# Token columns reordered and padded: prompts first, samples behind them, 272 columns per chunk instead of 264

## The chip, the cores and the metric

The kernel runs on one core of a Trainium2 chip. The metric is the device time of one execution in microseconds. Three executions of the kernel before took 560.51, 561.38 and 562.12 us; their median, 561.38 us, is the time that the change is compared with.

## The reference: what is computed

One inference step of a decoder layer for 256 prompt tokens and 8 sample tokens with 1024 channels, all in float32. All 264 tokens share the weights, so the large products are done once for both groups.

```python
x = x + 0.5 * swiglu_ffn(x, ffn1_norm, ffn1_w_in, ffn1_w_out)     # 1024 -> 2*2816 -> 1024
h = rmsnorm(x, mix_norm)
u, q, k, v, qm = split(h @ w_in)                                  # 1024 -> 2048
y_pool = pool_mixer(u, ...)                                       # windows 2, 4, 8, 16
y_moba = moba_attention(rotary(rmsnorm(q)), k_past + k, v_past + v)   # 8 heads x 64
y_mem  = mem_attention(rmsnorm(qm), mk, mv)                       # 256 memory tokens, 4 heads
x = x + concat(y_pool, y_moba, y_mem) @ w_out                     # 1024 -> 1024
x = x + 0.5 * swiglu_ffn(x, ffn2_norm, ffn2_w_in, ffn2_w_out)
```

Besides x, the new keys and values, the memory keys and values and the pooling state are returned.

## The kernel before

**Activations lie transposed.** Channels are on the 128 partitions and tokens along the free dimension, so 1024 channels are 8 chunks of `[128, 264]` in `xT`, `x_hi` and `x_lo`, and the 2816 hidden channels are 22 such chunks in `h_hi` and `h_lo`. In each chunk the 8 samples are columns 0 to 7 and the 256 prompts columns 8 to 263.

**Each float32 product is three matmuls.** A value is split into a rounded part (`_hi`, type float32r) and the rest (`_lo`). `three` (lines 1505 to 1507) issues hi·hi, hi·lo and lo·hi into the same PSUM accumulation. ScalarE makes `w_hi` from the loaded weights `raw` (line 701), VectorE makes `w_lo` (line 1021).

**Units of weights.** The weights come in 512 KB units into a ring of four slots of `[128, 1024]`, each unit used in this way:

- FFN in (`ffn_unit`, 44 units in each FFN): eight weight blocks of 128 columns are the stationary operands, one for each of the eight x chunks, and the x chunk of 264 columns is the moving operand: 8 x 3 = 24 matmuls into one PSUM bank. The moving operand goes on to the next chunk every three matmuls. The first FFN takes the chunks in the order 0 to 7, the second in the order 4, 5, 6, 7, 0, 1, 2, 3 (`M_ORDER`). Two units of the second FFN, at its start, take the hi products of all chunks first (lines 1531 to 1535).
- FFN out (`outer`, 22 units in each FFN): one h chunk is the moving operand for all 24 matmuls of a unit, while the eight weight blocks and the eight PSUM banks change. The last two units are interleaved (`last_two`).
- The output projection of the mixer ("MIX", 8 units) is of the same kind, with x chunks in the order 0, 1, 4, 5, 6, 7 and then 2 and 3 interleaved.
- Memory keys and values: 48 matmuls in which memory chunks of 128 columns (`m_hi`, `m_lo`) are stationary and the weights, 512 columns wide, are moving.
- The projection `w_in` of the prompts (`project`, 192 matmuls): the same with x as the stationary operand: a block of 128 prompts, from column 8 or 136 of a chunk. Between these stand the products of the samples and of the attention.

**Order and waits.** All five engines run instruction streams written out by hand and tied by counted semaphores; in the middle part a table `EXTRA` and a list `TAIL` say what is placed between the projection's steps. The change leaves both alone. TensorE waits for `lo_ready` before a unit, ScalarE for `w_used` before it writes a ring slot again.

**Where the tensors lie.** `place` gives each tensor a byte offset in the partition, counted up from 1152 and rounded to 64. From the shapes: `raw` 1152, `w_hi` 17536, `w_lo` 33920, `xT` 50304, `x_hi` 58752, `x_lo` 67200, `m_lo` 141696, `m_hi` 149888, `h_hi` 181952, `h_lo` 205184. A chunk of 264 float32 columns is 1056 bytes, that is 16.5 times 64, so chunk k of `x_hi` starts at byte 58752 + 1056 k. Weight blocks of 128 columns (512 bytes) all have the same remainder in a division by 256.

**The per-token norm of the mixer** (step "SS"): TensorE sums squares over the partitions, into column 0 of a PSUM bank for the samples (once in each quarter of the partitions) and into columns 1 and 2 for the prompts, and ScalarE and VectorE take root and reciprocal of the whole 128 x 3 block.

Of the kernel before, what the change touches and what calls it, by code (L numbers as in the profile page):

```python
# [13 lines left out]
ds = bass.ds  # L14
# [7 lines left out]
NP = 256  # L22
N = NS + NP
POOL, MOBA, MEM = 256, 512, 256
HD = 64
# [85 lines left out]
def layer(nc, a):  # L111

    ctx = ExitStack()
    with ctx:
        cursor = [1152]

        def place(name, shape, dt=F32, at=None):
            size = 4 * int(np.prod(shape[1:]))
            if at is None:
                at = cursor[0]  # L120
                cursor[0] += -(-size // 64) * 64
            return nc.alloc_sbuf_tensor_at(name, list(shape), dt, offset=at)
# [46 lines left out]
        dummy = place("dummy", [P, 4])  # L169
        ms = place("ms", [P, 2])  # L170
        m_root = place("m_root", [P, 2])
        m_rstd = place("m_rstd", [P, 2])
        t_root = place("t_root", [P, 3])
        t_rstd = place("t_rstd", [P, 3])
        x_ss = place("x_ss", [P, 3])
        x_root = place("x_root", [P, 3])
        x_rstd = place("x_rstd", [P, 3])
        page_ids = place("page_ids", [1, NS * PAGES], I32)
# [14 lines left out]

        late_slot = place("late_slot", [P, PAGES * 512], at=cursor[0])
        q_cols = place("q_cols", [P, 4 * 513])
        region = cursor[0]
        late_end = region + 4 * PAGES * 512 - (-(-4 * 4 * 513 // 64) * 64)
# [109 lines left out]
        ALL, MEM_ROWS = slice(0, P), slice(64, P)  # L307


        def cols_view(w, k):  # L310
# [383 lines left out]
        def _(act):  # L694
# [196 lines left out]
            for what, k in steps():  # L891
# [54 lines left out]
                elif what == "HY":  # L946
                    c0 = (2, 4, 6)[k]
                    act.wait_ge(pv_done, 2 * k + 2)
                    act.activation(x_hi[:, c0:c0 + 2, NS:N], bank[HY_BANKS[k]].rearrange("p (c n) -> p c n", c=2), ACT.Copy).then_inc(hy_hi, 1)
                elif what == "A" and k == 3:  # L950
# [11 lines left out]
                elif what == "M" and k == 0:  # L962
                    act.wait_ge(smn_ready, 1)
                    act.activation(rows_m[:], bank[QM_BANK][:, 0:NP], ACT.Exp, scale=SCALE, bias=m_stats[:, 1:2],
                                   accum_out=m_stats[:, 2:3]).then_inc(sme_ready, 1)
                elif what == "M" and k == 2:
                    act.wait_ge(p_psum, 1)
                    act.activation(pm_cols[:].rearrange("p t c -> p (t c)"), bank[QM_BANK][:, 0:NP], ACT.Copy).then_inc(pcols_ready, 1)
                elif what == "YR":
                    act.wait_ge(v_used, V_DONE[k])  # L970
                    if k:
                        act.wait_ge(yr_psum, k)
                    if k < 2:
                        act.wait_ge(s_total, 1)
                        act.activation(y_rows_s[:], bank[V_BANKS[k]][:, :], ACT.Copy, scale=stats[:, 64 + k:65 + k]).then_inc(yr_ready, 1)
                    else:
                        act.activation(y_rows_s[:], bank[QM_BANK][:, :], ACT.Copy).then_inc(yr_ready, 1)
                elif what == "CAT":
                    act.wait_ge(ys_ready, 4 + 2 * k)
                    c0, c1 = ((2, 6), (6, 8))[k]  # L980
                    act.activation(x_hi[:, c0:c1, 0:NS], ys[:, c0:c1, :], ACT.Copy).then_inc(cat_hi, 1)
            for r in range(4, KT + 1):
# [17 lines left out]
            act.wait_ge(res_ready, 3 * KT)  # L1000
            act.activation(xs[:], xT[:, :, 0:NS], ACT.Copy).then_inc(xs_copied, 1)
            y_rows(act, 2)
# [5 lines left out]
        def _(vec):  # L1008
# [25 lines left out]
            def residual(inst, last, weight, g0):  # L1034
# [7 lines left out]
                for idx, m in enumerate(M_ORDER):  # L1042
# [6 lines left out]
                    if g0 is None and idx < 4:  # L1049
                        vec.wait_ge(res_ready, KT * inst + idx + 1)  # L1050
                        vec.transpose(y_square(idx), xT[:, m, NS:N]).then_inc(y_squares, 1)
                    if g0 is not None and idx:
# [9 lines left out]
            def up_hidden(f, c, s, n, b0=GU_BANK, split_of=None):  # L1062
# [3 lines left out]
                if split_of is not None:  # L1066
# [4 lines left out]
                vec.wait_ge(hm_ready, c + (HT * f + 1))  # L1071
                vec.tensor_copy(h_hi[:, ds(c, 1), :].rearrange("p a n -> p (a n)"), h_tmp[:, s, :]).then_inc(hhi_ready, 1)
                vec.wait_ge(hhi_ready, c + (HT * f + 1))
                vec.tensor_tensor(h_lo[:, ds(c, 1), :].rearrange("p a n -> p (a n)"), h_tmp[:, s, :],  # L1074
                                  h_hi[:, ds(c, 1), :].rearrange("p a n -> p (a n)").bitcast(F32), ALU.subtract)\
                    .then_inc(h_ready, 1)
# [245 lines left out]
            for what, k in steps():  # L1322
# [127 lines left out]
                elif what == "HY":  # L1450
                    c0 = (2, 4, 6)[k]
                    vec.wait_ge(hy_hi, k + 1)
                    vec.tensor_tensor(x_lo[:, c0:c0 + 2, NS:N], bank[HY_BANKS[k]].rearrange("p (c n) -> p c n", c=2),
                                      x_hi[:, c0:c0 + 2, NS:N].bitcast(F32), ALU.subtract).then_inc(hy_lo, 1)
                elif what == "POOL" and k == 1:
# [20 lines left out]
                elif what == "CAT":  # L1476
                    vec.wait_ge(cat_hi, k + 1)
                    c0, c1 = ((2, 6), (6, 8))[k]
                    vec.tensor_tensor(x_lo[:, c0:c1, 0:NS], ys[:, c0:c1, :], x_hi[:, c0:c1, 0:NS].bitcast(F32), ALU.subtract).then_inc(cat_lo, 1)
            for r in range(4, KT + 1):  # L1480
# [21 lines left out]
        def _(pe):  # L1502
# [36 lines left out]
            def row_norms():  # L1539

                for t in range(3):
                    n, c0 = (NS, P, P)[t], (0, NS, NS + P)[t]
                    pe.wait_ge(xwide_ready, t + 1)
# [22 lines left out]

            hidden = lambda k: tuple(h[:, ds(k, 1), :].rearrange("p a n -> p (a n)") for h in (h_hi, h_lo))

# [57 lines left out]
            def project_samples(r):  # L1626
# [81 lines left out]
            def sample_turns(half):  # L1708
                for m in range(4 * half, 4 * half + 4):
                    turn(bank[X_BANKS[m]][:, 0:NS], x_rows[0:NS, 0, m * P:(m + 1) * P], NS)  # L1710

            def prompt_turns(half):
                pe.wait_ge(x_loaded[half], 32)
                for m in range(4 * half, 4 * half + 4):
                    turn(bank[X_BANKS[m]][:, NS:NS + P], x_rows[:, 1, m * P:(m + 1) * P])
                    turn(bank[X_BANKS[m]][:, NS + P:N], x_rows[:, 2, m * P:(m + 1) * P]).then_inc(x_turned, 1)

# [49 lines left out]
            for what, k in steps():  # L1767
# [26 lines left out]
                elif what == "SS":  # L1794
                    pe.wait_ge(sum_step, KT - 1)
                    pe.wait_ge(qkT_ready, 1)
                    for q in range(4):
                        pe.matmul(bank[SS_BANK][32 * q:32 * q + 32, 0:1], tmp[:, M_ORDER[0], 0:32], ones[:, 0:1], start=True, stop=True)
                    for tt in (1, 2):
                        c0 = (0, NS, NS + P)[tt]  # L1800
                        mm = pe.matmul(bank[SS_BANK][:, tt:tt + 1], tmp[:, M_ORDER[0], c0:c0 + P], ones[:, 0:1], start=True, stop=True)
# [26 lines left out]
                elif what == "POOL" and k == 0:  # L1828
# [3 lines left out]
                    for pr in range(2):  # L1832
# [3 lines left out]
                        for g, r, u0, u1 in pair:  # L1836
                            pe.matmul(out[r, NS:NS + P], u0, band[:, g, 0:P], start=True, stop=True)
                        for g, r, u0, u1 in pair:
                            pe.matmul(out[r, NS + P:N], u1, band[:, g, P + EDGE:], start=True, stop=False)
                        for g, r, u0, u1 in pair:  # L1840
                            pe.matmul(out[r, NS + P:NS + P + EDGE], u0, band[:, g, P:P + EDGE], start=False, stop=True)
                        for g, r, u0, u1 in pair:
                            mm = pe.matmul(out[r, 0:NS], ext[:, g * HD:(g + 1) * HD], samp[:, g, :], start=True, stop=True)
                        mm.then_inc(pooled_psum, 1)
# [118 lines left out]
            for pair in range(2):  # L1963
                for q in range(2):
                    pe.wait_ge(res_ready, 2 * KT + 4 + (2 if pair == 0 else 3 + q))
                    for t in range(2):
                        mm = turn(bank[Y_BANKS[2 * pair + t]][:, q * P:(q + 1) * P], xT[:, 2 * pair + q, NS + t * P:NS + (t + 1) * P])
                        if q:
# [31 lines left out]
```

## Time and profile before

| | |
|---|---|
| median of three executions | 561.38 us (560.51 to 562.12) |
| span of the profiled execution, first to last instruction | 559.2 us |
| TensorE matmuls | busy 551.3 us (99%), 5075 of them |
| TensorE weight loads | 513.6 us (92%) |
| VectorE, ScalarE, GpSimd | 398.9 us (71%), 269.2 us (48%), 17.7 us (3%) |
| granted TensorE clock | 1.000 |
| DMA | 128.40 MB, mean 230 GB/s |

The profiled execution's own device time is not listed apart from its span. The span lies 2.2 us under the median, which is what lies around it when it is taken as one execution like the three.

The duration that the profile gives for a matmul runs from its issue to its last result. Matmuls overlap: the next one starts long before the last has ended. What a matmul costs in a dense stretch is the distance from its start to the start of the next, and this is read from the timeline, whose first column is the start; the busy time of a group divided by its count says nothing about it.

### The profile page before, as it was taken

How to read it: one execution, taken by the hardware profiler on the slowest of the kernel's cores; microseconds unless marked ns; L12 is line 12 of the kernel's file. 1: busy time of each engine (PE TensorE's matmuls, PEld its weight loads, DVE VectorE, ACT ScalarE, POOL GpSimd, SP SyncE). 2: the span in 40 equal slices, each digit the busy share in tenths (PEclk: the TensorE clock that was granted, in tenths of full speed). 3: DMA queues.
4: the chain of work that ended last, by engine and by line, in shares of the span. 5: the costliest groups of instructions: out<-in, count | busy, mean ns of one | idle time of the engine just before them, and what ended most of it. 6: DMA issues, size and time to landing. Idle time of an engine off the chain costs nothing.

```text
span 559.2 us, 13391 instructions
## 1 busy us (share of the span) xinstructions
PE 551.3 (99%) x5075; PEld 513.6 (92%) x5075; DVE 398.9 (71%) x715; ACT 269.2 (48%) x425; POOL 17.7 (3%) x24
## 2 busy tenths in 40 slices
PE   8999999999999999999999999999999999999997
PEld 8999999999899998666777679999999999999997
DVE  4687888885588877889946685689777777664444
ACT  5844464444543337344535785475444344433330
POOL 1000000000000003100000000140000000000000
PEclk9999999999999999999999999999999999999999
DMA  9799999784567664899999994566756666465523
GB/s 236 208 269 324 271 315 268 234 249 149 196 216 273 205 209 160 273 338 382 351 300 371 373 337 143 163 180 197 211 168 191 182 175 194 132 220 181 187 75 79
DMA packets 137481, 128.40 MB, mean 230 GB/s; under 512 B 10937, under 2 KB 108880, under 8 KB 137432
## 3 DMA queue, kind: packets, MB, share of 16 engines
q1 hardware_dynamic: 134703, 127.24, 72.8%
q10 hardware_dynamic: 2736, 0.61, 0.5%
q8 instruction: 26, 0.43, 0.3%
q14 instruction: 16, 0.12, 0.1%
HBM read 125.12 MB, written 2.83 MB: 229 GB/s over the span
## 4 chain that ended last, share of the span: by engine, by line
PE 85%; DVE 7%; DMA 3%; ACT 2%; issue 1%; SPq 0%; DVEq 0%; ACTq 0%
PE banks L1505 25%; PE banks L1506 25%; PE banks L1507 25%; PE banks L1665 3%; PE banks L1513 2%; DVE w_lo L1021 2%; PE banks L1939 1%; PE banks L1637 1%; DMA raw<-in_ffn_w_in 1%; PE banks L1890 1%; DMA x_rows<-in_x_sample 1%; DMA page_ids<-in_page_table 1%; PE banks L1866 1%; ACT x_hi L827 1%; DVE prob_pair L1448 1%
## 5 line engine op out<-in xcount | busy, mean ns | idle before, releaser
L701 ACT ACTIVATE w_hi<-raw 128x1024 fp32r<-128x1024 f32 x158 | 166.5, 1059 | 194.9 <-PE banks L1507 160.8
L1021 DVE TENSOR_TENSOR w_lo<-raw,w_hi 128x1024 fp32r<-128x1024 f32 x158 | 193.8, 1232 | 73.9 <-ACT w_hi L701 72.7
L1505 PE MATMUL banks<-x_hi,w_hi 128*128 128x264 f32 x752 | 214.1, 285 | 0.1
L1506 PE MATMUL banks<-x_lo,w_hi 128*128 128x264 f32 x752 | 213.0, 283 | 0.0
L1507 PE MATMUL banks<-x_hi,w_lo 128*128 128x264 f32 x752 | 213.0, 283 | 0.0
L1505 PEld LDWEIGHTS banks<-x_hi,w_hi 128*128 128x128 f32 x752 | 141.6, 188 | 0.7 <-issue 0.4
L1506 PEld LDWEIGHTS banks<-x_lo,w_hi 128*128 128x128 f32 x752 | 141.7, 188 | 0.0
L1507 PEld LDWEIGHTS banks<-x_hi,w_lo 128*128 128x128 f32 x752 | 141.0, 188 | 0.0
L1505 PE MATMUL banks<-h_hi,w_hi 128*128 (+1 forms) x352 | 100.2, 285 | 0.0
L1507 PE MATMUL banks<-h_hi,w_lo 128*128 (+1 forms) x352 | 100.2, 285 | 0.0
L1506 PE MATMUL banks<-h_lo,w_hi 128*128 (+1 forms) x352 | 100.0, 284 | 0.0
L1506 PEld LDWEIGHTS banks<-h_lo,w_hi 128*128 128x128 f32 x352 | 66.5, 189 | 0.0
L1505 PEld LDWEIGHTS banks<-h_hi,w_hi 128*128 128x128 f32 x352 | 66.2, 188 | 0.3 <-ACT mem_kv L879 0.3
L1507 PEld LDWEIGHTS banks<-h_hi,w_lo 128*128 128x128 f32 x352 | 66.3, 188 | 0.0
L1065 DVE TENSOR_TENSOR h_tmp<-banks,rstd 128x264 f32<-128x264 f32 x44 | 18.9, 429 | 22.7 <-PE banks L1507 22.7
L1032 DVE STREAM_TRANSPOSE kv<-kv 128x1024 f32<-128x1024 f32 x28 | 33.9, 1228 | 0.0
L1505 PE MATMUL banks<-w_hi,x_hi 128*128 128x512 f32 x64 | 28.0, 438 | 0.3 <-ACT qp L794 0.3
L726 ACT ACTIVATE sg<-sg 128x264 f32<-128x264 f32 x44 | 18.3, 415 | 18.2 <-DVE sg L1060 18.2
L1507 PE MATMUL banks<-w_hi,x_lo 128*128 128x512 f32 x64 | 25.3, 395 | 0.0
L1506 PE MATMUL banks<-w_lo,x_hi 128*128 128x512 f32 x64 | 25.2, 394 | 0.0
L1074 DVE TENSOR_TENSOR h_lo<-h_tmp,h_hi 128x264 f32 (+1 forms) x44 | 19.1, 434 | 3.6
L1070 DVE TENSOR_TENSOR h_tmp<-sg,h_tmp 128x264 f32<-128x264 f32 x44 | 19.0, 433 | 3.3 <-ACT sg L726 2.0
(287 smaller groups left out, 501.7 us busy)
## 6 DMA issues: line engine op xcount, KB each, us to landing
raw<-in_ffn_w_in SPq DMA_DIRECT2D x86, 512.0 KB, 4.8
raw<-in_ffn_w_out SPq DMA_DIRECT2D x44, 512.0 KB, 3.4
kv<-in_cache_k SPq DMA_DIRECT2D x56, 256.0 KB, 4.8
kv<-in_cache_v SPq DMA_DIRECT2D x48, 256.0 KB, 6.3
raw<-in_w_in SPq DMA_DIRECT2D x12, 512.0 KB, 5.2
late_slot<-in_cache_v SPq DMA_DIRECT2D x16, 256.0 KB, 4.6
raw<-in_w_out SPq DMA_DIRECT2D x8, 512.0 KB, 7.5
raw<-in_mem_w_kv SPq DMA_DIRECT2D x4, 512.0 KB, 4.0
```

The costliest lines, as they stand in the source:

```text
L701: act.activation(w_hi[:, n % RING, :], raw[:, n % RING, :], ACT.Copy).then_inc(hi_ready, 1)
L726: act.activation(sg[:, s, :], sg[:, s, :], ACT.Silu).then_inc(silu_ready, 1)
L1021: vec.tensor_tensor(w_lo[:, n % RING, :], raw[:, n % RING, :], w_hi[:, n % RING, :].bitcast(F32), ALU.subtract).then_inc(lo_ready, 1)
L1032: vec.transpose(key_pair(g), key_pair(g)).then_inc(k_turned8, 1)
L1065: vec.tensor_tensor(h_tmp[:, s, :], bank[b0 + 2 * s + 1][:, 0:N], rstd[:], ALU.mult).then_inc(gu_free, 1)
L1070: vec.tensor_tensor(h_tmp[:, s, :], sg[:, s, :], h_tmp[:, s, :], ALU.mult).then_inc(hm_ready, 1)
L1074: vec.tensor_tensor(h_lo[:, ds(c, 1), :].rearrange("p a n -> p (a n)"), h_tmp[:, s, :], h_hi[:, ds(c, 1), :].rearrange("p a n -> p (a n)") ...
L1505: pe.matmul(out, lhs[0], rhs[0], start=start, stop=False)
L1506: pe.matmul(out, lhs[0], rhs[1], start=False, stop=False)
L1507: return pe.matmul(out, lhs[1], rhs[0], start=False, stop=stop)
L1513: return pe.transpose(out, in_, ident[0:k, 0:k])
L1665: mm = pe.matmul(bank[LG_BANK][32 * hp:32 * hp + 32, half * NP:(half + 1) * NP], q_cols[:, c0:c0 + 32], keys[:, 4 * hp + c], start=(b4 == ...
```

## The change

Prompts are now columns 0 to 255 of each chunk and the samples columns 256 to 263. The chunks of `x_hi`, `x_lo`, `h_hi` and `h_lo` lie 272 columns (1088 bytes, 17 times 64) apart, while still 264 columns are computed; `xT` and `tmp` keep 264. `place` rounds to 32 bytes rather than 64 and counts two bytes for a bfloat16, and eight small tensors share one, to make room. Which columns each instruction reads or writes follows from this everywhere. One instruction is added: VectorE sets column 0 of the norm's PSUM bank to one, because the samples' sum is now written to 8 rows of each quarter rather than to 32.

New offsets that matter here: `x_hi` 58752 and the three weight tensors as before, `x_lo` 67456, `h_hi` 181440, `h_lo` 205376.

```diff
+PITCH = 272
+PROMPT, SAMPLE = slice(0, NP), slice(NP, N)
+TOKENS = ((NP, NS), (0, P), (P, P))
...
-            size = 4 * int(np.prod(shape[1:]))
+            size = (2 if dt == BF16 else 4) * int(np.prod(shape[1:]))
             if at is None:
                 at = cursor[0]
-                cursor[0] += -(-size // 64) * 64
+                cursor[0] += -(-size // 32) * 32
...
-        x_hi = place("x_hi", [P, KT, N], F32R)
-        x_lo = place("x_lo", [P, KT, N], F32R)
+        x_hi = place("x_hi", [P, KT, PITCH], F32R)[:, :, 0:N]
+        x_lo = place("x_lo", [P, KT, PITCH], F32R)[:, :, 0:N]
...
-        h_hi = place("h_hi", [P, HT, N], F32R)
-        h_lo = place("h_lo", [P, HT, N], F32R)
+        h_hi = place("h_hi", [P, HT * PITCH], F32R)
+        h_lo = place("h_lo", [P, HT * PITCH], F32R)
...
+        def hidden_of(h, c):
+
+            return h[:, ds(c * PITCH, N)]
...
+            vec.memset(bank[SS_BANK][:, 0:1], 1.0).then_inc(xs_ready, 1)
             vec.memset(bank[S_BANK][:, 0:P], 0.0).then_inc(xs_ready, 1)
             vec.wait_ge(res_ready, KT)
-            vec.tensor_tensor(xs[:], xT[:, :, 0:NS], gains[:, 8:16].unsqueeze(2).to_broadcast([P, KT, NS]), ALU.mult).then_inc(xs_ready, 1)
+            vec.tensor_tensor(xs[:], xT[:, :, SAMPLE], gains[:, 8:16].unsqueeze(2).to_broadcast([P, KT, NS]), ALU.mult).then_inc(xs_ready, 1)
...
-            hidden = lambda k: tuple(h[:, ds(k, 1), :].rearrange("p a n -> p (a n)") for h in (h_hi, h_lo))
+            hidden = lambda k: (hidden_of(h_hi, k), hidden_of(h_lo, k))
...
-                k, c0 = 2 * J_ORDER[r] + kk, (0, NS, NS + P)[tt]
+                k, c0 = 2 * J_ORDER[r] + kk, TOKENS[tt][0]
...
-                    pe.wait_ge(xs_ready, 2)
+                    pe.wait_ge(xs_ready, 3)
...
-                        pe.matmul(bank[SS_BANK][32 * q:32 * q + 32, 0:1], tmp[:, M_ORDER[0], 0:32], ones[:, 0:1], start=True, stop=True)
+                        pe.matmul(bank[SS_BANK][32 * q:32 * q + NS, 0:1], tmp[:, M_ORDER[0], SAMPLE], ones[:, 0:1], start=True, stop=True)
```

The instruction streams stay the same but for two places. On VectorE, behind the residual of the first FFN and ahead of the split of the projection's third weight unit, the kernel before has (banks are PSUM, `xs` the samples' columns):

```order
L1039 SCALAR_TENSOR_TENSOR x_lo<-xT,gains,x_hi 128x264 x2
L1315 MEMSET banks 128x128
L1317 TENSOR_TENSOR xs<-xT,gains 128x64
L1021 TENSOR_TENSOR w_lo<-raw,w_hi 128x1024
L1330 MEMSET q_spread 128x128
```

and the changed one:

```order
L1045 SCALAR_TENSOR_TENSOR x_lo<-xT,gains,x_hi 128x264 x2
L1320 MEMSET banks 128x1
L1321 MEMSET banks 128x128
L1323 TENSOR_TENSOR xs<-xT,gains 128x64
L1027 TENSOR_TENSOR w_lo<-raw,w_hi 128x1024
L1336 MEMSET q_spread 128x128
```

One memset of a single column has come in; nothing has moved past another. On TensorE, in the third step of the projection, where the squares are summed, there stood

```order
L1507 MATMUL banks<-w_hi,x_lo 128x512
L1818 MATMUL banks<-q_spread,joined 128x128
L1798 MATMUL banks<-ones,tmp 32x1 x4
L1801 MATMUL banks<-ones,tmp 128x1 x2
L1505 MATMUL banks<-w_hi,x_hi 128x512
```

and now stands

```order
L1513 MATMUL banks<-w_hi,x_lo 128x512
L1824 MATMUL banks<-q_spread,joined 128x128
L1804 MATMUL banks<-ones,tmp 8x1 x4
L1807 MATMUL banks<-ones,tmp 128x1 x2
L1511 MATMUL banks<-w_hi,x_hi 128x512
```

The same six matmuls, four of them over 8 rows in place of 32. All other rows of TensorE and VectorE differ in their line numbers alone.

## Rows read from the trace of the kernel before

**Rows 1.** Clock of the core; busy time of TensorE and its weight loads.

```profile
core 0: 559.2 us, clock 1.000
PE 551.3 (99%) x5075; PEld 513.6 (92%) x5075; DVE 398.9 (71%) x715; ACT 269.2 (48%) x425; POOL 17.7 (3%) x24
```

**Rows 2.** Page: the chain that ended last, by engine.

```profile
PE 85%; DVE 7%; DMA 3%; ACT 2%; issue 1%; SPq 0%; DVEq 0%; ACTq 0%
```

**Rows 3.** The page's costliest TensorE group.

```profile
L1505 PE MATMUL banks<-x_hi,w_hi 128*128 128x264 f32 x752 | 214.1, 285 | 0.1
```

**Rows 4.** Timeline of TensorE (start us, duration us, ...): second FFN in, 36 units apart.

```profile
382.79 0.28 PE L1505 MATMUL banks<-x_hi,w_hi 128*128 128x264 f32 x1
...
487.19 0.28 PE L1505 MATMUL banks<-x_hi,w_hi 128*128 128x264 f32 x1
```

**Rows 5.** Timeline: first matmuls of MIX chunks 4, 5, 6, 7, 2, and the next stage.

```profile
344.47 0.28 PE L1505 MATMUL banks<-x_hi,w_hi 128*128 128x264 f32 x1
...
347.35 0.28 PE L1505 MATMUL banks<-x_hi,w_hi 128*128 128x264 f32 x1
...
350.27 0.28 PE L1505 MATMUL banks<-x_hi,w_hi 128*128 128x264 f32 x1
...
353.17 0.29 PE L1505 MATMUL banks<-x_hi,w_hi 128*128 128x264 f32 x1
...
356.06 0.28 PE L1505 MATMUL banks<-x_hi,w_hi 128*128 128x264 f32 x1
...
361.91 0.28 PE L1505 MATMUL banks<-x_hi,w_hi 128*128 128x264 f32 x1
```

**Rows 6.** Timeline, second FFN out: first matmuls of h chunks 2 to 10.

```profile
495.94 0.29 PE L1505 MATMUL banks<-h_hi,w_hi 128*128 x1
...
498.92 0.29 PE L1505 MATMUL banks<-h_hi,w_hi 128*128 x1
...
501.85 0.28 PE L1505 MATMUL banks<-h_hi,w_hi 128*128 x1
...
504.77 0.28 PE L1505 MATMUL banks<-h_hi,w_hi 128*128 x1
...
507.70 0.28 PE L1505 MATMUL banks<-h_hi,w_hi 128*128 x1
...
510.61 0.29 PE L1505 MATMUL banks<-h_hi,w_hi 128*128 x1
...
513.51 0.28 PE L1505 MATMUL banks<-h_hi,w_hi 128*128 x1
...
516.41 0.28 PE L1505 MATMUL banks<-h_hi,w_hi 128*128 x1
...
519.34 0.29 PE L1505 MATMUL banks<-h_hi,w_hi 128*128 x1
```

**Rows 7.** Timeline, 512 columns moving: memory product (first, next stage); projection (first, next).

```profile
140.17 0.40 PE L1505 MATMUL banks<-w_hi,m_hi 128*128 128x512 f32 x1
...
151.06 0.28 PE L1505 MATMUL banks<-h_hi,w_hi 128*128 128x264 f32 x1
...
215.81 0.40 PE L1505 MATMUL banks<-w_hi,x_hi 128*128 128x512 f32 x1
...
218.61 0.60 PE L1513 MATMUL banks<-ident,mem_kv 128*128 128x128 f32 x4
```

**Rows 8.** Timeline of VectorE and TensorE around the added memset.

```profile
219.28 0.17 DVE L1315 MEMSET banks<- 128x128 f32 x1
219.35 0.21 DVE L1317 TENSOR_TENSOR xs<-xT,gains 128x64 f32<-128x64 f32 x1
219.71 1.23 DVE L1021 TENSOR_TENSOR w_lo<-raw,w_hi 128x1024 fp32r<-128x1024 f32 x1
...
220.53 1.93 PE L1637 MATMUL banks<-raw,xs 128*8 128x128 f32 x64
...
223.87 0.39 PE L1505 MATMUL banks<-w_hi,x_hi 128*128 128x512 f32 x1
```

More of the change, by code:

```diff
@@ L169, in layer @@
         dummy = place("dummy", [P, 4])
[L170 to L177, printed above, removed]
+        norms_of = place("norms_of", [P, 24])
+        ms, m_root, m_rstd = norms_of[:, 0:2], norms_of[:, 2:4], norms_of[:, 4:6]
+        t_root, t_rstd = norms_of[:, 6:9], norms_of[:, 9:12]
+        x_ss, x_root, x_rstd = norms_of[:, 12:15], norms_of[:, 15:18], norms_of[:, 18:21]
         page_ids = place("page_ids", [1, NS * PAGES], I32)
@@ L980, in _ @@
                     c0, c1 = ((2, 6), (6, 8))[k]
-                    act.activation(x_hi[:, c0:c1, 0:NS], ys[:, c0:c1, :], ACT.Copy).then_inc(cat_hi, 1)
+                    act.activation(x_hi[:, c0:c1, SAMPLE], ys[:, c0:c1, :], ACT.Copy).then_inc(cat_hi, 1)
             for r in range(4, KT + 1):
@@ L1071, in up_hidden @@
                 vec.wait_ge(hm_ready, c + (HT * f + 1))
[L1072 removed]
+                vec.tensor_copy(hidden_of(h_hi, c), h_tmp[:, s, :]).then_inc(hhi_ready, 1)
                 vec.wait_ge(hhi_ready, c + (HT * f + 1))
[L1074 to L1075 removed]
+                vec.tensor_tensor(hidden_of(h_lo, c), h_tmp[:, s, :], hidden_of(h_hi, c).bitcast(F32), ALU.subtract)\
                     .then_inc(h_ready, 1)
@@ L1452, in _ @@
                     vec.wait_ge(hy_hi, k + 1)
-                    vec.tensor_tensor(x_lo[:, c0:c0 + 2, NS:N], bank[HY_BANKS[k]].rearrange("p (c n) -> p c n", c=2),
-                                      x_hi[:, c0:c0 + 2, NS:N].bitcast(F32), ALU.subtract).then_inc(hy_lo, 1)
+                    vec.tensor_tensor(x_lo[:, c0:c0 + 2, PROMPT], bank[HY_BANKS[k]].rearrange("p (c n) -> p c n", c=2),
+                                      x_hi[:, c0:c0 + 2, PROMPT].bitcast(F32), ALU.subtract).then_inc(hy_lo, 1)
                 elif what == "POOL" and k == 1:
@@ L1478, in _ @@
                     c0, c1 = ((2, 6), (6, 8))[k]
-                    vec.tensor_tensor(x_lo[:, c0:c1, 0:NS], ys[:, c0:c1, :], x_hi[:, c0:c1, 0:NS].bitcast(F32), ALU.subtract).then_inc(cat_lo, 1)
+                    vec.tensor_tensor(x_lo[:, c0:c1, SAMPLE], ys[:, c0:c1, :], x_hi[:, c0:c1, SAMPLE].bitcast(F32), ALU.subtract).then_inc(cat_lo, 1)
             for r in range(4, KT + 1):
@@ L1541, in row_norms @@
                 for t in range(3):
[L1542 removed]
+                    c0, n = TOKENS[t]
                     pe.wait_ge(xwide_ready, t + 1)
@@ L1836, in _ @@
                         for g, r, u0, u1 in pair:
-                            pe.matmul(out[r, NS:NS + P], u0, band[:, g, 0:P], start=True, stop=True)
+                            pe.matmul(out[r, 0:P], u0, band[:, g, 0:P], start=True, stop=True)
                         for g, r, u0, u1 in pair:
-                            pe.matmul(out[r, NS + P:N], u1, band[:, g, P + EDGE:], start=True, stop=False)
+                            pe.matmul(out[r, P:NP], u1, band[:, g, P + EDGE:], start=True, stop=False)
                         for g, r, u0, u1 in pair:
-                            pe.matmul(out[r, NS + P:NS + P + EDGE], u0, band[:, g, P:P + EDGE], start=False, stop=True)
+                            pe.matmul(out[r, P:P + EDGE], u0, band[:, g, P:P + EDGE], start=False, stop=True)
                         for g, r, u0, u1 in pair:
-                            mm = pe.matmul(out[r, 0:NS], ext[:, g * HD:(g + 1) * HD], samp[:, g, :], start=True, stop=True)
+                            mm = pe.matmul(out[r, SAMPLE], ext[:, g * HD:(g + 1) * HD], samp[:, g, :], start=True, stop=True)
                         mm.then_inc(pooled_psum, 1)
```

23 lines of the change are left out of this document (13 added, 10 removed).

## The prediction, made blind

> **What bounds the kernel now.** I read the page's busy line first: TensorE is busy for 99% of the span, at a granted clock of 1.000 throughout, which is the upper of its two levels, 2.4 GHz [rows 1]. The chain that ended last is TensorE for 85% [rows 2]. So the end moves with the distance between two matmul starts and with nothing else, and I want that distance, not the 285 ns that the group of line 1505 shows, which overlap [rows 3].
>
> The timeline gives it. In the second FFN's first product 36 units of 24 matmuls take 487.19 - 382.79 = 104.40 us: 2.900 us a unit, 120.8 ns a matmul [rows 4]. 264 columns at 2.4 GHz are 110 ns, so 10.8 ns of each matmul is something else. The reader is to see next that this rest is not the same everywhere, though all these matmuls have the same shape and none waits. With one x chunk as moving operand for 24 matmuls, chunk 4 takes 2.88 us, chunk 5 2.92, chunk 6 2.90, chunk 7 2.89 [rows 5]. With h chunks it is 2.98, 2.93, 2.92, 2.93, 2.91, 2.90, 2.90, 2.93 for chunks 2 to 9 [rows 6]. What differs between these units is the chunk's start address. Where the weights are moving, 512 columns wide, 48 matmuls against memory chunks take 151.06 - 140.17 = 10.89 us, 226.9 ns each, and 12 against x chunks 218.61 - 215.81 = 2.80 us, 233.3 ns each [rows 7]; there the stationary operand's address differs.
>
> **The addresses.** Take the start byte modulo 256 (a modulus that I choose because the weights all have remainder 128 in it, and 1056 = 4 x 256 + 32 then gives a period of 8 chunks). Before, x_hi and x_lo chunk k both have 128 + 32k; h_hi chunk c has 192 + 32c and h_lo 128 + 32c. So MIX chunk 4 has 0, chunk 5 has 32, chunk 6 has 64, chunk 7 has 96. The h chunks 2, 4, 6, 8 start at multiples of 64 in both parts, but the two parts lie 64 apart in remainder, and each `three` steps from one to the other and back. Afterwards x_hi and x_lo have 128 + 64k, h_hi 192 + 64c, h_lo 64 + 64c: every operand starts at a multiple of 64, the x parts always agree, and the h parts differ by 128.
>
> **Part by part.** The sum is made against the profiled execution: 559.2 us of span and 2.2 us around it, which is the median of 561.4 us shown.
>
> 1. FFN in, 88 units. The clean case with one chunk and a multiple of 64 is 2.88 us (chunk 4). The two odd chunks average 2.905 us. A unit of FFN in is half one and half the other: 2.8925 us if nothing else counted; it takes 2.900, so eight steps from chunk to chunk cost 7.5 ns together. Afterwards no odd chunks are left: 2.88 + 0.0075 = 2.8875, a gain of 12.5 ns in each of 88 units, 1.1 us. Ends: all at 2.88 gives 1.8 us; for the other end I take what steps of 64 cost in h. The four aligned h chunks take 2.98 + 2.92 + 2.91 + 2.90 = 11.71 us, 2.93 on average, 50 ns over 2.88 for 16 steps of 64, about 3 ns each; the worst, chunk 2, 100 ns, 6.3 ns each. Eight such steps make 2.904 or 2.930: a loss of 0.4 or of 2.6 us. I take 1.1, since the nearest rows are x chunks whose two parts agree.
> 2. FFN out, 44 units. The average over eight h chunks is (519.34 - 495.94) / 8 = 2.925 us. The four odd ones add up to 11.69 us, the aligned to 11.71: alignment to 64 alone gives h nothing, and that speaks against the change. What is new is that the parts lie 128 apart rather than 64, and no row shows that. Bounds: 2.88 (parts agree), a gain of 2.0 us, and 2.98 (the worst aligned chunk), a loss of 2.4 us. I take 2.915, a gain of 10 ns a unit, 0.4 us, near to the average that both kinds have now.
> 3. MIX, 8 units: chunk 5 gives back 0.04 us, chunk 7 0.01, chunk 1 I price as chunk 5 (0.04), and chunks 2 and 3, interleaved, take 361.91 - 356.06 = 5.85 us where two clean units take 5.76; I take 0.07 of the 0.09. Together 0.16 us, between 0 and 0.2.
> 4. Projection, 192 matmuls: 233.3 against 226.9 ns makes 1.2 us if x as stationary operand becomes as good as the memory chunks. These start at remainder 128 like the weights; x chunks will for k = 0 and 4 only. I take 0.5 us, between 0 and 1.2.
> 5. The memset on VectorE: the one that stands there is 0.17 us long, and the next instruction starts 0.07 us behind its start [rows 8]. Behind it are `xs`, done at 219.56 and first read by TensorE at 220.53, and `w_lo` of the third unit, done at 220.94 and first read at 223.87 [rows 8]. So 0.97 and 2.93 us of TensorE's other work hide it: nothing. Without that cover it would be 0.1 to 0.2 us. The four sums over 8 rows instead of 32, and the moved columns of copies, transposes and stores, keep their number and shape: nothing.
>
> Sum: 1.1 + 0.4 + 0.16 + 0.5 = 2.2 us less. 559.2 - 2.2 = 557.0 us of span, 559.2 us of time.
>
> As VectorE and ScalarE have slack (71% and 48% busy, rows 1), a faster TensorE is not held up by the splits: a unit of 2.89 us holds one split of 1.23 us on VectorE [rows 8].
>
> **The rivals.**
>
> A. *All of it goes*: whatever costs more than 2.88 us a unit and 226.9 ns is due to unaligned starts. For: chunk 4 is at 2.88 exactly, and memory chunks, all aligned, at 226.9. Against: the aligned h chunks are no faster than the others. 1.8 + 2.0 + 0.2 + 1.2 = 5.2 us: 556.2 us.
>
> B. *The address doesn't decide*: the spread comes from what the other engines do at that moment or from the order of the matmuls, and the padding changes nothing. For: chunk 6 starts aligned and takes 2.90. Against: in FFN out every unit gives the other engines the same work, one split each, and yet chunks 2 and 3 differ by 0.05 us [rows 6]. 561.4 us. The Trainium skill ("TensorE: Matmul & The Clock Gate", Back-to-back issue gap) has a rule in which the address has no place: the gap is N/2.4 + 2.5 ns. For 264 columns that would be 112.5 ns, before and after alike; the trace has 120.8 and does not agree. Its "SBUF — State Buffer" (Door 1: The DMA port swizzle) speaks of lines of 16 bytes, with a penalty for each line crossed. 1056 and 1088 bytes are both whole multiples of 16, so by that rule too the change would bring nothing; the difference between chunks 4 and 5 does not agree with it.
>
> C. *The new steps are worse than the odd starts*: each change of the moving operand's remainder, by 64 from chunk to chunk in FFN in and by 128 between h_hi and h_lo, costs what h chunk 2 shows. Its place is FFN out: every unit at 2.98 costs 2.4 us; with FFN in at 2.904 another 0.4, less 0.66 from the projection and MIX: 563.5 us. It decides, with these other terms, from the point where an FFN-out unit takes 2.97 us, since 44 x 0.045 + 0.4 - 0.66 is the 1.7 us that can be told from nothing. For: the slowest unit of all has two aligned parts, at 0 and 192. Against: the other three aligned chunks.
>
> **How the numbers follow.** Forecast 0.50, A 0.18, B 0.21, C 0.11. A difference under 0.3%, 1.7 us, can't be told from none here: faster means under 559.7, slower over 563.1. The forecast's own spread (FFN out alone is uncertain by 2 us each way) puts three quarters of it under 559.7: 0.37, with A 0.55. Same: the rest of the forecast 0.12, B 0.21 and a part of C 0.02, 0.35. Slower: the bulk of C, and a little of the forecast: 0.10. The range of 8 in 10 reaches nearly to A and half way to C: 556.3 to 562.2 us.
>
> **What would show it.** In the changed kernel's timeline: FFN-in units at 2.88 to 2.89 us apart (2.90: B; over 2.90: C); FFN-out units with a period of four chunks instead of eight, around 2.915; all MIX units at 2.88; projection matmuls under 232 ns; the memory product still 226.9, as nothing about it changes; `xs` done before TensorE asks for it. The prediction is wrong if units are above 2.90 anywhere in FFN in, or if FFN out stays at 2.925 on average, or if span and unit times don't add up, because then something other than matmul distance has moved.

## The result: 0.4% slower, and the profile after

Six executions of the changed kernel took 562.63 to 565.04 us, median 563.62, beside 561.75 us for the kernel before, measured together with it: ratio 1.0041, 95% interval 1.0026 to 1.0056. A second set of the same kernel later gave 1.0049 (1.0036 to 1.0062). The change costs about 2.5 us. I had forecast 559.2 us with a range up to 562.2, and a chance of 0.10 for slower. The prediction is wrong in its direction. It also took differences under 0.3% for too small to be told from none; the intervals here reach about 0.15% to each side.

The page of the changed kernel, whose profiled execution took 562.63 us, reads at first like the one before [rows 1 to 3]:

```profile
core 0: 560.8 us, clock 1.000
PE 554.1 (99%) x5075; PEld 516.6 (92%) x5075; DVE 399.1 (71%) x716; ACT 269.6 (48%) x425; POOL 17.7 (3%) x24
PE 93%; DVE 5%; ACT 1%; issue 1%; POOL 0%; DVEq 0%; POOLq 0%
L1511 PE MATMUL banks<-x_hi,w_hi 128*128 128x264 f32 x752 | 215.3, 286 | 0.0
```

Same clock, same count of matmuls, 2.8 us more busy time on TensorE and, with 6.7 us in place of 7.9, no more idle time: so the matmuls themselves lie farther apart. The timeline says where. Its rows (start, duration) at the borders of the stages are, before:

```profile
15.70 0.28 PE L1505 MATMUL banks<-x_hi,w_hi 128*128 128x264 f32 x1
...
376.99 0.28 PE L1505 MATMUL banks<-x_hi,w_hi 128*128 128x264 f32 x1
...
490.09 0.28 PE L1505 MATMUL banks<-h_hi,w_hi 128*128 128x264 f32 x1
...
545.73 0.29 PE L1505 MATMUL banks<-h_hi,w_hi 128*128 128x264 f32 x1
```

and after:

```profile
14.96 0.36 PE L1511 MATMUL banks<-x_hi,w_hi 128*128 128x264 f32 x1
...
150.76 0.28 PE L1511 MATMUL banks<-h_hi,w_hi 128*128 128x264 f32 x1
...
215.51 0.39 PE L1511 MATMUL banks<-w_hi,x_hi 128*128 128x512 f32 x1
...
344.19 0.28 PE L1511 MATMUL banks<-x_hi,w_hi 128*128 128x264 f32 x1
...
361.77 0.29 PE L1511 MATMUL banks<-x_hi,w_hi 128*128 128x264 f32 x1
...
376.86 0.29 PE L1511 MATMUL banks<-x_hi,w_hi 128*128 128x264 f32 x1
...
491.78 0.29 PE L1511 MATMUL banks<-h_hi,w_hi 128*128 128x264 f32 x1
...
547.40 0.29 PE L1511 MATMUL banks<-h_hi,w_hi 128*128 128x264 f32 x1
```

With [rows 5] and [rows 7] for the borders in between, the differences are:

| stage | before, us | after, us | change |
|---|---|---|---|
| start to the third FFN-in unit | 15.70 | 14.96 | -0.74 |
| rest of first FFN in, and memory product | 135.36 | 135.80 | +0.44 |
| first FFN out | 64.75 | 64.75 | 0 |
| projection to MIX chunk 4 | 128.66 | 128.68 | +0.02 |
| MIX chunks 4 to 7, 2 and 3 | 17.44 | 17.58 | +0.14 |
| second FFN in, first 5 units, with the norm | 15.08 | 15.09 | +0.01 |
| second FFN in, other 39 units | 113.10 | 114.92 | +1.82 |
| second FFN out, 19 units | 55.64 | 55.62 | -0.02 |
| its last 3 units and the rest | 13.47 | 13.40 | -0.07 |
| span | 559.2 | 560.8 | +1.6 |

The first row is the start-up: 0.74 us of luck in this execution. The first product starts at 8.96 us here and at 9.78 before, and in the profiles of experiments 2, 7, 8 and 9, which have the same token order and x pitch, anywhere from 8.71 to 9.91. The second row holds some luck too: one unit, from 39.4 us on before and 38.8 after, took 3.18 and 2.96 us, with a pause of TensorE in it. Without the first row the change costs 2.34 us here, and 1.82 of that is second FFN in: 114.92 / 39 = 2.947 us a unit, against 2.900 before. By the rhythm of a unit I mean the time from its first matmul's start to the next unit's, with the 24 distances that it is made of. In the first FFN the same code with the same addresses runs in two rhythms. Timeline, first FFN in, first matmuls of units:

```profile
59.34 0.29 PE L1511 MATMUL banks<-x_hi,w_hi 128*128 128x264 f32 x1
...
77.02 0.29 PE L1511 MATMUL banks<-x_hi,w_hi 128*128 128x264 f32 x1
...
84.62 0.29 PE L1511 MATMUL banks<-x_hi,w_hi 128*128 128x264 f32 x1
...
136.94 0.29 PE L1511 MATMUL banks<-x_hi,w_hi 128*128 128x264 f32 x1
```

Six units in 77.02 - 59.34 = 17.68 us are 2.947 us each; 18 units in 136.94 - 84.62 = 52.32 us are 2.907 each. Between the two stand 16 transposes of memory rows. Within a rhythm every unit repeats the same 24 distances (120 to 127 ns in the slow one, 116 to 123 in the quick one) to a nanosecond or two; before there is only one rhythm, 2.900 (distances of 116 to 129 ns), in both FFNs.

The units from 44.77 to 56.39 us took 2.90 to 2.91 us as well, and what stands between these and the slow ones is no other matmul. Timeline of TensorE's matmuls, then of its weight loads, where the unit of 56.39 begins:

```profile
56.27 0.28 PE L1513 MATMUL banks<-x_hi,w_lo 128*128 128x264 f32 x1
56.39 0.30 PE L1511 MATMUL banks<-x_hi,w_hi 128*128 128x264 f32 x1
56.53 0.28 PE L1512 MATMUL banks<-x_lo,w_hi 128*128 128x264 f32 x1
```

```profile
56.16 0.19 PEld L1513 LDWEIGHTS banks<-x_hi,w_lo 128*128 128x128 f32 x1
56.30 0.19 PEld L1511 LDWEIGHTS banks<-x_hi,w_hi 128*128 128x128 f32 x1
```

and of VectorE just ahead of it:

```profile
54.61 1.23 DVE L1027 TENSOR_TENSOR w_lo<-raw,w_hi 128x1024 fp32r<-128x1024 f32 x1 [3.50 <-ACT w_hi L707]
55.75 0.43 DVE L1071 TENSOR_TENSOR h_tmp<-banks,rstd 128x264 f32<-128x264 f32 x1
```

The first weight load of this unit starts 27 ns behind the start of the matmul before it; in all other units from 44 to 137 us but the one behind the transposes it is 3 or 4 ns. One distance of 135 ns in place of 123 follows, a unit of 2.950 us, and then the slow rhythm. The unit's wait for `gu_free` is released by the second VectorE row, which ends at 56.18 us, 0.12 us ahead of the load; VectorE had stood 3.50 us waiting for ScalarE's `w_hi` shortly before (first row). So in this place a delay of some 20 ns, from another engine, was followed by the change of rhythm; no run repeats it by itself.

FFN out has the period of four chunks that I expected. Timeline, chunks 2 to 5 of the second FFN:

```profile
497.64 0.29 PE L1511 MATMUL banks<-h_hi,w_hi 128*128 x1
...
500.57 0.29 PE L1511 MATMUL banks<-h_hi,w_hi 128*128 x1
...
503.50 0.28 PE L1511 MATMUL banks<-h_hi,w_hi 128*128 x1
...
506.42 0.28 PE L1511 MATMUL banks<-h_hi,w_hi 128*128 x1
```

2.93, 2.93, 2.92 and (from there on) 2.93: 2.927 on average, where before had 2.925 [rows 6].

### The profile page after: what moved, and what is told of

It reads as the page before. It is cut to its first block, busy times and chain, and to the rows that moved or that the text cites. A ratio compares the mean times of both kernels' runs of the same rounds, so it can differ in the third digit from the quotient of the medians.

```text
span 560.8 us, 13392 instructions
## 1 busy us (share of the span) xinstructions
PE 554.1 (99%) x5075; PEld 516.6 (92%) x5075; DVE 399.1 (71%) x716; ACT 269.6 (48%) x425; POOL 17.7 (3%) x24
## 4 chain that ended last, share of the span: by engine, by line
PE 93%; DVE 5%; ACT 1%; issue 1%; POOL 0%; DVEq 0%; POOLq 0%
PE banks L1511 27%; PE banks L1513 27%; PE banks L1512 26%; PE banks L1519 3%; PE banks L1671 3%; PE banks L1945 1%; PE banks L1643 1%; PE banks L1712 1%; PE banks L1896 1%; PE banks L1872 1%; DVE w_lo L1027 1%; DVE prob_pair L1454 1%; DVE banks L1441 0%; DVE kp L1142 0%; DVE mx L1444 0%
```

## The experiments

**1 to 3. One part alone.** The pitch was split in two, `X_PITCH` for x_hi and x_lo and `H_PITCH` for h_hi and h_lo; all else as in the changed kernel.

```diff
-PITCH = 272
+X_PITCH, H_PITCH = 264, 264        # order only
+X_PITCH, H_PITCH = 272, 264        # x pitch
+X_PITCH, H_PITCH = 264, 272        # h pitch
```

> The changed kernel with both pitches back at 264; the token order, the packing of small tensors and the added memset stay. Theory P (the start addresses of the x chunks as moving operand carry the loss): FFN-in units at 2.900 us in both FFNs, FFN-out units with the old period of eight and 2.98 us for h chunks 2 and 10, time as before, ratio within 0.3% of 1. Rival T (the token order, the moved columns or the memset carry it): ratio 1.003 to 1.005 with units still near 2.90 and the loss in the stretch between the FFNs.

> The changed kernel with the pitch of h back at 264 and that of x left at 272. Theory P: FFN-in units as in the changed kernel, 2.907 or 2.947 us, those of the second FFN at 2.947, which is 42 x 0.047 = 2.0 us there and 0.3 to 2 in the first; ratio about 1.004, as the whole change. Rival H (the h pitch carries the loss): ratio within 0.2% of 1. Rival O (the slower units come from ScalarE, VectorE or DMA traffic that happens to meet TensorE's reads): the two values of a unit need not come back; others between 2.90 and 2.95, uneven from unit to unit.

> The changed kernel with the pitch of x back at 264 and that of h left at 272. Theory P: FFN-in units at 2.900 us, FFN-out units at 2.92 to 2.93 with a period of four, ratio within 0.2% of 1. Rival H: ratio about 1.004.

Measured beside 561.06 us before: order only 561.0 us, ratio 0.9998 (0.9988 to 1.0009); x pitch 563.74 us, 1.0049 (1.0034 to 1.0064); h pitch 561.0 us, 0.9993 (0.9982 to 1.0004). The two borders of second FFN in, order only:

```profile
376.50 0.28 PE L1511 MATMUL banks<-x_hi,w_hi 128*128 128x264 f32 x1
...
489.60 0.28 PE L1511 MATMUL banks<-h_hi,w_hi 128*128 128x264 f32 x1
```

x pitch:

```profile
376.99 0.29 PE L1511 MATMUL banks<-x_hi,w_hi 128*128 128x264 f32 x1
...
491.91 0.29 PE L1511 MATMUL banks<-h_hi,w_hi 128*128 128x264 f32 x1
```

h pitch:

```profile
377.10 0.28 PE L1511 MATMUL banks<-x_hi,w_hi 128*128 128x264 f32 x1
...
490.20 0.28 PE L1511 MATMUL banks<-h_hi,w_hi 128*128 128x264 f32 x1
```

113.10, 114.92 and 113.10 us: the whole loss of that stage comes with the pitch of x and with nothing else. Token order, packing, the memset and the h pitch are all neutral, within the 0.1 to 0.2% that these intervals allow. In the four other profiles with the x pitch of 272 (experiments 2, 7, 8 and 9) the units from the sixth of this stage on take 2.947 as well, up to the place where experiment 7 puts something in; in the profiles with 264 (before, 1, 3, 6 and 10) they take 2.900.

**4. Matmuls alone, by address.** A kernel without the layer (its outputs are zeros, the layer is left out), called the bench below: TensorE issues groups of the same triples with chosen start bytes, never waiting, and from 60 us on no other engine is busy. "Remainder" is the start byte modulo 256; all weights have 128, as in the real kernel. A walk is a unit whose moving operand goes on to the next of eight chunks every three matmuls. In short form:

```diff
+def same(ph, pl, units):      # one moving chunk for 24 matmuls, remainders ph and pl of its two parts
+def chunks(step, base, units) # next of 8 chunks every three matmuls, as in FFN in
+SECTIONS = [same(32*p, 32*p, 2) ...] + [same(32*p, 32*q, 1) ...] + [chunks(1024 + 32*s, 128, 3) for s in 1..8]
```

> A kernel of matmuls alone: operands are made once, then TensorE runs 264-column matmuls back to back with no wait, no other engine and no DMA beside it; its outputs are zeros, the layer is left out. Sections of 48 matmuls with one moving chunk whose two parts start at remainder 0, 32, ..., 224 modulo 256; sections of 24 for all 64 pairs of remainders of the two parts; and FFN-in patterns with eight chunks 1056, 1088, ..., 1280 bytes apart. Theory P: the unit times of the real kernels come back by address alone: 2.88 us at equal remainder 0, 2.92 at 32, 2.98 for the pair (0, 192), 2.90 for the pitch of 1056 and 2.91 or 2.95 for 1088; and 2.88 for 1280, where nothing moves modulo 256. Rival O (other engines' traffic): every section has the same time, 2.88 us or less for 24 matmuls. Rival N (columns alone, a fixed gap): the same, whatever the address.

The section with a pitch of 1056 bytes and the next, with 1088. Timeline, where equal matmuls are joined into one row; of the 72 of each section the window takes 44:

```profile
281.41 5.47 PE L204 MATMUL banks<-mv,w 128*128 128x264 f32 x44
...
290.13 5.57 PE L204 MATMUL banks<-mv,w 128*128 128x264 f32 x44
```

A matmul's own 0.28 us taken off, 5.19 / 43 = 120.7 ns and 5.29 / 43 = 123.0 ns apart. By starts, the last two units of each section were (us; for one chunk, the last unit, by the one border or the other):

```
pitch   1056   1088   1120   1152   1184   1216   1248   1280
unit    2.900  2.947  2.913  2.920  2.927  2.933  2.920  2.912-2.918
one chunk only, both parts at remainder (modulo 256)
        0      32     64     96     128    160    192    224
unit    2.880  2.920  2.880  2.880  2.909-2.917  2.933  2.903  2.920
```

2.900 and 2.947 are the real kernels' values, with the same 24 distances in the same order. So matmuls and addresses alone make these values, with next to no DMA traffic, no VectorE and no wait beside them; this strikes the first half of my rival B, that the other engines make the spread. It does not say that they can't pick between the two rhythms, as VectorE's late release at 56.18 us seems to have done. Two of my expectations were missed. With 1280 bytes every chunk has remainder 128, and the walk takes 2.912 to 2.918, not 2.88; but one chunk that stays put at 128 takes 2.909 to 2.917, so the walk adds nothing there, and what was wrong is that I took the 2.88 of remainder 0 for 128. And the pair at 0 and 192, h chunk 2 of the kernel before, took 2.933 in its single unit, not 2.98. The 64 pairs ran one unit each, from 2.880 to 2.965, each right behind another pair: the pair at 0 and 0 took 2.965 there and 2.880 in its own section. So they say little about a pair by itself.

**5. Distances, disturbances, widths.** Again matmuls alone, outputs zeros; shortened, two other orders of the chunks and some sections with fixed weights or a fixed moving operand follow.

```diff
+SECTIONS  = [chunks(1056, 128, 3, 16384 + 64*j) for j in range(16)]    # distance of the two parts
+SECTIONS += [chunks(1088, 128, 3, 16384 + 128*j) for j in range(8)]
+SECTIONS += [nudge(n, times) + chunks(1088, 128, 3, 16384 + 512) for n, times in
+             ((128, 1), (128, 2), (64, 3), (512, 1), (256, 2), (32, 5))]
+SECTIONS += [same(0, 0, 2, n) for n in (256, 264, 272, 512)]
```

> Matmuls alone again, outputs zeros, the layer left out. FFN-in patterns of eight chunks (24 matmuls) with the two parts of x 0, 64, ..., 960 bytes apart modulo 1024 at pitch 1056, and 0, 128, ..., 896 at pitch 1088; pitch 1088 behind six different short disturbances; two other orders of the chunks; one pair of operands 256, 264, 272 and 512 columns wide; and matmuls in which only the weights move on, or only the moving operand. Theory P2 (addresses decide, but the same addresses can settle in more than one rhythm, and what came just before picks it): pitch 1088 at distance 512 gives 2.907 behind some disturbances and 2.947 behind others; some distance at pitch 1088 stays under 2.90 and some at 1056 above it. Rival P1 (address alone, one time for each): 2.947 behind every disturbance, and the 2.907 of the real kernel comes from other engines. Rival S (alignment to 64 is good by itself, the loss is the distance of the parts): pitch 1088 is faster than 1056 at the best distance of each.

At 1056 the distance between the parts matters: 0, 64, 128, 192 modulo 256 give 2.900, 2.927, 2.904 to 2.923 and 2.907, and this repeats four times. At 1088 eight distances all give 2.907, none under 2.90, where I had expected some to be, so at the best distance of each the old pitch is the quicker one. In two other orders of the chunks 1056 gives 2.907 to 2.918 and 1088 gives 2.903 to 2.930. With one weight block for all matmuls and only the moving operand walking, the two pitches give 2.900 and 2.906: the moving operand's walk alone makes these values. Behind one matmul of 128 columns, two of 128, three of 64 or one of 512 the same walk runs at 2.947, and at 2.907 behind two of 256 or five of 32. Behind one of 512, and behind two of 256, 47 matmuls each:

```profile
283.95 5.93 PE L225 MATMUL banks<-mv,w 128*128 128x264 f32 x47
...
292.88 5.86 PE L225 MATMUL banks<-mv,w 128*128 128x264 f32 x47
```

5.65 / 46 = 122.8 ns against 5.58 / 46 = 121.3 ns. It holds its rhythm from the second unit to the end of the section, two units. Of the six disturbances only two changed what ran before them: one of 128 columns (2.907 before, 2.947 behind) and two of 256 (2.947, then 2.907). The other four stood behind a walk that already had the rhythm that is found behind them, so whether they set it or left it alone isn't known.

With the moving operand at remainder 0, 264 columns cost 120.0 ns, 256 cost 118.7, 272 cost 126.7 and 512 cost 232.5. But the very same 48 matmuls of 264 columns, as the first section of this run, settled at 2.960 a unit in place of 2.880, so a unit whose operand stays put has two rhythms as well.

**6. Padding the other way.** In the kernel before, the start of h_lo was moved up so that both h parts have the same remainder, and the pitch stayed.

```diff
         h_hi = place("h_hi", [P, HT, N], F32R)
+        cursor[0] += 64
         h_lo = place("h_lo", [P, HT, N], F32R)
```

> The kernel before with 64 unused bytes ahead of h_lo, so that both parts of an h chunk start at the same remainder modulo 256; nothing else changes. Theory P, by the table of remainder pairs measured with matmuls alone: equal remainders average 2.910 us a unit over eight chunks, the pairs of the kernel before 2.925, so 44 units gain 0.7 us: ratio 0.9985 to 0.9995, units between 2.88 and 2.935. Rival P2 (the rhythm that a unit falls into depends on what came before): unit times differ from the table by up to 0.05 us either way, and the sum lies anywhere within 1 us of before. Rival Z (the distance of h parts has no effect): 2.925 on average with 2.98 at chunks 2 and 10.

560.94 us beside 561.15, ratio 0.9996 (0.9986 to 1.0007). The units of eight chunks, from chunk 1 on, became 2.915, 2.964, 2.923, 2.911, 2.885, 2.915, 2.925, 2.902: 2.9175 on average, against 2.926, so 44 x 8 ns = 0.4 us, too little to show in the time. The average moved by half of the 15 ns that the table of pairs had promised, and single chunks didn't follow the table: chunk 2, both parts at remainder 0, takes 2.964, outside the expected 2.88 to 2.935.

**7 to 9. Switching the rhythm in the real kernel.** In the changed kernel, inside second FFN in, two matmuls over 256 columns are put in whose result is thrown away; then two over 128 as a control; and the changed kernel once more as it is.

```diff
-            ffn_in_loop(1, 3, HT // 2)
+            ffn_in_loop(1, 3, 5)
+            pe.wait_ge(gu_free, HT + 4)
+            for _ in range(2):
+                pe.matmul(bank[0][:, 0:256], x_hi[:, 0, 0:P], x_hi[:, 6, 0:256], start=True, stop=True)
+            ffn_in_loop(1, 5, HT // 2)
```

> The changed kernel with two extra matmuls of 256 columns (0.24 us, their result is not used) between two iterations in the middle of the second FFN's first product. Theory P2 (two rhythms for the same addresses, picked by what came before): as with matmuls alone, where two such matmuls behind the 2.947 rhythm gave 2.907, the units behind them, some 24 of them, take 2.907 in place of 2.947, 1.0 us less, and about 0.7 us less in all than the changed kernel. Rival P1 (the real kernel's 2.947 belongs to the second FFN: chunk order, or the other engines there): 2.947 ahead and behind, 0.2 us more in all.

> The same with two matmuls of 128 columns in place of 256. Theory P2: with matmuls alone two of these left the 2.947 rhythm as it was, so the units stay at 2.947 and the time is that of the changed kernel plus 0.1 us. Rival G (any interruption resets it): 2.907 behind them too.

> The changed kernel once more, as the measure for the two others. Ratio to before 1.003 to 1.006; units of the second FFN's first product at 2.947, those of the first at 2.907 or 2.947, h units with a period of four around 2.927.

With 256 columns, the extra pair, the second unit behind it and the end of the stage:

```profile
421.61 0.40 PE L1970 MATMUL banks<-x_hi 128*128 128x256 f32 x2
...
424.76 0.29 PE L1511 MATMUL banks<-x_hi,w_hi 128*128 128x264 f32 x1
...
491.61 0.29 PE L1511 MATMUL banks<-h_hi,w_hi 128*128 128x264 f32 x1
```

66.85 us for 23 units: 2.907 each, where every unit from the sixth of the stage to 421.61 took 2.947. With 128 columns:

```profile
422.58 0.34 PE L1970 MATMUL banks<-x_hi 128*128 128x128 f32 x2
...
425.73 0.29 PE L1511 MATMUL banks<-x_hi,w_hi 128*128 128x264 f32 x1
...
493.50 0.29 PE L1511 MATMUL banks<-h_hi,w_hi 128*128 128x264 f32 x1
```

67.77 us for 23 units: 2.947, unchanged. Both came out as in the bench: two matmuls of 256 columns took the walk from the slow rhythm to the quick one, two of 128 did not, although the same wait stands ahead of both pairs. Each was seen in one execution in the kernel and in one of the bench. The times were 562.96, 564.52 and 563.67 us beside 560.79 before (ratios 1.0035, 1.0065, 1.0049, each within 0.0016), but they can't be set against one another by this edit alone, since the first FFN ran in different mixtures: from about 85 us on at 2.947 in both kernels with extra matmuls (long before these ran), at 2.907 in the unchanged one. Up to there the three kernels are the same, and the same 16 transposes stand ahead of the 2.907 of one and the 2.947 of the others: which matmuls stand ahead does not fix the rhythm by itself. That mixture is worth up to 40 x 0.04 = 1.6 us, of the 2.4 us between the changed kernel's six times. That the spread comes from there is argued from the unit times; only one execution of each kernel shows them.

**10. h pitch and agreement together.** As experiment 3, with `cursor[0] += 128` ahead of `h_lo`, so that h_hi and h_lo agree and all h chunks start at multiples of 64: the best case by my reasoning.

```diff
         h_hi = place("h_hi", [P, HT * H_PITCH], F32R)
+        cursor[0] += 128
         h_lo = place("h_lo", [P, HT * H_PITCH], F32R)
```

> The changed kernel with the x pitch back at 264, the h pitch at 272 and h_lo moved on by 128 bytes, so that both parts of every h chunk start at the same multiple of 64 modulo 256. It is the version that would beat both kernels if the table of pairs from matmuls alone held: equal remainders 0, 64, 128 and 192 took 2.88 to 2.90 us a unit there once settled, with one slower rhythm of 2.96 at 0. Optimistic theory: units average 2.885, 44 x 0.04 = 1.8 us less, ratio 0.997. Theory P2: the rhythm is handed on from the unit before, and in the run with h pitch 264 and equal remainders the aligned chunks averaged 2.923; then units lie between 2.88 and 2.96 with 2.92 on average and the ratio within 0.1% of 1.

561.14 us beside 561.18, ratio 0.9994 (0.9980 to 1.0007). The four kinds of chunk take 2.907, 2.961, 2.918 and 2.921: 2.927 on average, the same as with parts 128 apart, and nowhere near 2.88. None of the kernels is faster than the one before by more than can be measured.

## Why the prediction was wrong, step by step

**What bounds the kernel: right.** TensorE's start-to-start distance sets the end; every change of the span is a change of distances, and what came late or early besides is the start-up and one pause in the first FFN.

**Term 1, FFN in: the step that failed.** I priced a unit at 2.8875 us, a gain of 1.1 us over both FFNs; it is 2.907 or 2.947, a loss of 1.82 in the second FFN and, with the pause and the memory product in it, 0.44 in the first. Three assumptions stood in it, each with its own fault. First, I took 2.88 as the property of an aligned address, from MIX chunk 4 [rows 5], a unit in which the moving operand stays put, and left chunk 6, aligned too and at 2.90, out. 2.88 is one of two rhythms of such a unit: the same matmuls at remainder 0 gave 2.880 and 2.960 in experiments 4 and 5, and aligned, agreeing h chunks gave 2.961 in experiment 10. Second, I charged the step from chunk to chunk with the 7.5 ns per unit that remained before; a step of 1088 bytes costs 27 or 67 ns over 2.880 in eight steps, 3.4 or 8.4 ns each. I had the right comparison in hand, the steps of 64 in h with 3 to 6.3 ns, and used it as the far end of the range; even that end, 2.930, was passed. The trace before could have warned me. In MIX chunk 6 [rows 5] the eleventh matmul starts at

```profile
351.50 0.28 PE L1506 MATMUL banks<-x_lo,w_hi 128*128 128x264 f32 x1
```

so the first ten take 351.50 - 350.27 = 1.23 us, up to 132 ns each, and the fourteen behind them 1.67 us, about 120 ns each. Behind a step of the moving operand more matmuls than the next three are slow, and in FFN in the next step comes after three. The bench has the same: one chunk at remainder 64 takes 2.906 us in its first unit and 2.880 in its second. Third, I assumed that one address pattern has one time. It has two. In the second FFN the first unit, from 361.77 on, takes 2.947, the one at 370.59 still 2.900, and behind the norm's matmul of 264 columns (373.49) come a unit of 3.12 with a pause in it and then, from 376.86 on, only 2.947. That the norm's matmul picks the slow one is likely by its place, but was not tried by itself.

**Term 2, FFN out: the mechanism had no effect.** Forecast 2.915, measured 2.927 against 2.925: 0 instead of -0.4 us. The sign against alignment that I had noted (aligned and odd h chunks equal in sum) was the one to follow.

**Term 3, MIX: wrong sign, small.** Chunks 4, 5, 6, 7:

```profile
344.19 0.28 PE L1511 MATMUL banks<-x_hi,w_hi 128*128 128x264 f32 x1
...
347.06 0.28 PE L1511 MATMUL banks<-x_hi,w_hi 128*128 128x264 f32 x1
...
349.97 0.28 PE L1511 MATMUL banks<-x_hi,w_hi 128*128 128x264 f32 x1
...
352.93 0.29 PE L1511 MATMUL banks<-x_hi,w_hi 128*128 128x264 f32 x1
```

The next starts at 355.85. Chunks 4 and 5 take 2.87 and 2.91 by these rows, of which I had hoped 2.88 for both; but 6 and 7 take 2.96 and 2.92, where before took 2.90 and 2.89 [rows 5]. Chunk 6 now starts at remainder 0, as chunk 4 did before: the same remainder in the same kind of unit, 2.88 then and 2.96 now. The six chunks lost 0.14 us where I had 0.16 gained for all eight.

**Term 4, projection: nothing, where I had 0.5 us.** The stage takes 128.68 us in place of 128.66. The first twelve matmuls against x take 218.30 - 215.51 = 2.79 us, 232.5 ns each, against 233.3 [rows 7]; my test was "under 232". Most x blocks still start where the memory chunks do not, but whether that holds them above 226.9 was not tried by itself.

**Term 5, memset and sums: right**, neutral in experiment 1.

**The rivals.** B's time is struck by experiment 2, and that the address doesn't decide by experiment 4; but what ran just before, and at 56.30 us what another engine did, picks between two rhythms, which is a part of B. A needed 2.88 in a walk of the moving operand, which no walk showed. C, with 0.11, was right about the kind (the steps are worse than the odd starts) and its time, 563.5, is within 0.2 us of the median; but it put 2.4 us into FFN out and 0.4 into FFN in, and measured were 0 and about 2.3. It came out at the right number from the wrong place. The Trainium skill ("TensorE: Matmul & The Clock Gate", Back-to-back issue gap) gives N/2.4 + 2.5 ns for an isolated matmul's gap, 112.5 ns for 264 columns, and names no address; experiments 4 and 5 have 120.0 to 123.3 ns (2.880 to 2.960 us for 24) by address and by what ran before, and do not agree.

**What stays open.** Why 1088 bytes has two rhythms and 1056 one, and which unit of storage or which buffer in front of TensorE produces them, no run here tells. That 1056 has only one is not shown by the bench, which put no disturbance ahead of it; in the real kernels every walk at 1056 came back to 2.900 within a few units, behind the norm's matmul, the transposes and the pauses, in all five profiles that have it. That two matmuls of 256 columns switch the rhythm and two of 128 do not is known for this walk alone, and the late weight load at 56.30 us says that a short delay with no other matmul may do it too, seen once.

## What to carry to other kernels

Starting every operand at a rounder address isn't a gain in itself: when TensorE is the bound, measure the start-to-start distance in the walk that the kernel really makes, with its step, since a unit whose operand stays put says little about one that moves on. Before changing a pitch, look at what the present one gives: an odd one may be the good one (here 1056 bytes, the best of eight), and matmuls alone in a small kernel reproduced the real distances to a nanosecond or two, so much of the question can be settled before the layout is rebuilt. Run each pattern there more than once and behind different neighbours, since one section shows one rhythm only. Where equal units show two times, compare what ran just ahead of them, and whether their first weight load came late, before looking for traffic.

## What the chip showed that I had not expected

- The same 24 matmuls at the same addresses run steadily at 2.907 or at 2.947 us, and can hold either for long: 39 units in second FFN in. Once a first weight load that came 27 ns behind the matmul before it, in place of 3 or 4, was followed by the change from one to the other.
- Two extra matmuls of 256 columns, 0.23 us in all, switched 2.947 to 2.907 for the next 23 units, which gives back 23 x 0.04 = 0.9 us, 0.7 net; two of 128 columns did not.
- Eight columns more or less don't cost in proportion: 256, 264, 272 columns with the moving operand at remainder 0 take 118.7, 120.0, 126.7 ns. The pitch of 272 is one thing, computing 272 columns would be a worse one.
- With the DMA engines busy for 99% and VectorE for 74% (59 to 77 us of the changed kernel) the distances equal, to a nanosecond or two, those of the bench, where both are idle.
